# Three-block diffusion kernel: the opening reordered, thirds loaded from GpSimd, context normed a block ahead, unused products added

## The reference

```python
mod   = silu(c)     @ w_ada + b_ada        # six parts of 1024: shift, scale, gate, shift, scale, gate
mod_c = silu(c_ctx) @ w_ada + b_ada
h_l = rms_norm(x,   g_mix) * (1 + scale)   + shift
h_c = rms_norm(ctx, g_mix) * (1 + scale_c) + shift_c
p_l, p_c = h_l @ w_in, h_c @ w_in          # 1024 x 3072; the context needs only columns 1024 to 2559
mix = [fourier_mix(u), recurrent(q, v, gates, state of the context)] @ w_out
x = x + gate * mix
x = x + gate2 * experts(...)               # 16 experts, 32 tokens each, all their weights are read
```

## Time and profile before

| | |
|---|---|
| median of 3 runs | 2242.82 us |
| profiled execution | 2239.62 us, its span 2237.8 us |
| granted TensorE clock, mean | 0.859 |
| PE busy | 1707.0 us (76%) |
| VectorE, ScalarE, GpSimd busy | 808.9, 514.3, 60.8 us |
| DMA | 760.71 MB, mean 340 GB/s |
| chain that ended last | DMA 50%, PE 42%, DVE 5%, ACT 1%, issue 1% |

### The profile page before, as it was taken

How to read it: one execution, slowest core, us unless ns; L and a number is a source line. 1 busy time by engine, 2 the same in 40 slices (tenths; PEclk the granted TensorE clock), 3 DMA queues, 4 the chain that set the end, 5 groups by cost and what they waited for, 6 DMA issues and landing times.

```text
span 2237.8 us, 33889 instructions
## 1 busy us (share of the span) xinstructions
PE 1707.0 (76%) x14906; PEld 1183.2 (53%) x14906; DVE 808.9 (36%) x1271; ACT 514.3 (23%) x833; POOL 60.8 (3%) x94
## 2 busy tenths in 40 slices
PE   5999986656565665665765666665999999999997
PEld 4897752312222321331322222232898999998997
DVE  5766731000100100100010010010875789688877
ACT  2420210000000000000000000000673664365664
POOL 0015000000000000000000000000000000000000
PEclk8998988777778777887777877777999999999998
DMA  9776989999999999999999999999645659753541
GB/s 360 292 261 266 380 345 431 431 432 432 432 431 432 432 431 433 431 431 432 431 433 433 431 432 431 433 432 415 221 143 207 198 161 360 260 170 124 168 133 67
DMA packets 139014, 760.71 MB, mean 340 GB/s; under 512 B 7943, under 2 KB 96775, under 8 KB 106920
## 3 DMA queue, kind: packets, MB, share of 16 engines
q1 hardware_dynamic: 135256, 754.13, 83.5%
q10 hardware_dynamic: 3664, 5.24, 0.7%
HBM read 756.20 MB, written 3.14 MB: 339 GB/s over the span
## 4 chain that ended last, share of the span: by engine, by line
DMA 50%; PE 42%; DVE 5%; ACT 1%; issue 1%; SPq 0%; DVEq 0%; ACTq 0%
DMA arena<-in_w_exp_up 25%; DMA arena<-in_w_exp_gate 24%; PE ps L854 19%; PE ps L1171 6%; PE ps L1308 4%; PE ps L805 3%; PE ps L727 2%; DMA arena<-in_w_in 1%; PE ps L1006 1%; PE ps L1289 1%; PE ps L848 1%; DVE ring_lo L1734 1%; PE ps L1217 1%; PE ps L910 0%; PE ps L1228 0%
## 5 line engine op out<-in xcount | busy, mean ns | idle before, releaser
L1171 PE MATMUL ps<-arena,const 128*32 128x352 f32 x2816 | 334.7, 635 | 248.2 <-DMA arena<-in_w_exp_up 128.9
L1171 PEld LDWEIGHTS ps<-arena,const 128*32 128x32 f32 x2816 | 105.4, 141 | 465.4 <-DMA arena<-in_w_exp_up 163.8
L854 PE MATMUL ps<-u_hi,w_hi 128*128 128x258 f32 x960 | 277.3, 289 | 1.3 <-DVE ring_lo L1734 1.1
L1734 DVE TENSOR_TENSOR ring_lo<-ring,w_hi 128x1024 fp32r<-128x1024 f32 x217 | 263.8, 1219 | 31.1 <-ACT w_hi L1359 29.7
L2139 DVE TENSOR_TENSOR tail<-tail,ps 128x704 f32<-128x704 f32 x15 | 13.3, 888 | 720.6 <-PE ps L1171 720.6
L854 PE MATMUL ps<-u_lo,w_hi 128*128 128x258 f32 x960 | 272.9, 284 | 0.0
L854 PE MATMUL ps<-u_hi,ring_lo 128*128 128x258 f32 x960 | 269.2, 280 | 0.0
L1359 ACT ACTIVATE w_hi<-ring 128x1024 fp32r<-128x1024 f32 x217 | 227.1, 1051 | 55.4 <-PE ps L1308 34.6
L1171 PE MATMUL ps<-ring,const 128*32 128x352 f32 x1024 | 125.5, 654 | 80.6 <-DMA ring<-in_w_exp_gate 40.9
L854 PEld LDWEIGHTS ps<-u_hi,w_hi 128*128 128x128 f32 x960 | 181.6, 189 | 7.3 <-issue 5.2
L854 PEld LDWEIGHTS ps<-u_hi,ring_lo 128*128 128x128 f32 x960 | 183.3, 191 | 0.0
(11 more groups left out here) (317 smaller groups left out, 2435.4 us busy)
## 6 DMA issues: line engine op xcount, KB each, us to landing
arena<-in_w_exp_gate SPq DMA_DIRECT2D x45, 2816.0 KB, 35.2
ring<-in_w_exp_down SPq DMA_DIRECT2D x31, 3072.0 KB, 33.0
arena<-in_w_exp_up SPq DMA_DIRECT2D x32, 2816.0 KB, 35.8
ring<-in_w_in SPq DMA_DIRECT2D x37, 1536.0 KB, 7.0
arena<-in_w_exp_down SPq DMA_DIRECT2D x16, 3072.0 KB, 36.3
ring<-in_w_exp_gate SPq DMA_DIRECT2D x15, 2816.0 KB, 30.8
ring<-in_w_exp_up SPq DMA_DIRECT2D x15, 2816.0 KB, 30.3
ring<-in_w_ada SPq DMA_DIRECT2D x24, 1536.0 KB, 7.6
```

What stands on the lines that cost most here:

```text
L854: m = pe.matmul(ps[:, bank, 0:a.shape[-1]], w, a, start=(k == 0 and j == 0), stop=(k == KD - 1 and j == 2))
L1171: m = pe.matmul(ps[32 * j:32 * j + 32, bank + h, 0:FJ // 2], XCUR[:, k, :], SPACE[at][:, a:a + FJ // 2], start=(k == 0), stop=(k == KD - 1 ...
L1734: tt(slot(c["u"], KD, c["w"], of=LOW_SLOT)[:, :, at], slot(c["u"], KD, c["w"])[:, :, at], w_hi[:, s % HI, :, :].bitcast(F32), ALU.subtract ...
```

## The change

1. `in1`'s first unit gets its own place (`IN1_AT`, in `arena` at 13 K), outside the ring; its low parts are written in place. SP issues its load between ada units 5 and 6. TensorE does six ada units ahead of the context's sum of squares (`FIRST_ADA`), ScalarE the first three high parts ahead of the rows, VectorE all three low parts ahead of `mod_in(0)`. The context's modulation values and scale are formed behind x's chunks.
2. The thirds are issued by GpSimd, the first three when block 0 of `in1` is done, the fourth (which lies in the first unit's place) when that unit has been used, the others each when its buffer is free. The 24 that aren't gate thirds are used two items later than before.
3. In items 0 to 7 one chunk of context is normed by VectorE a block ahead and modulated by ScalarE (`modulated_context`), its low part is taken an item later.
4. `fill` puts a turn off to its next call; level 7 has a fill too.
5. Unused products: four behind `first_turn`, seven of 128 columns ahead of level 1, two behind the ada unit at `o_diagonal`, four ahead of each output projection of the third block.

```diff
 IN2_AT = 11
+IN1_AT = 7
...
-THIRD_AT = sorted([(3 + n, n % THIRDS, n // THIRDS) for n in range(THIRDS * KD)] +
+THIRD_AT = sorted([(5 + n, n % THIRDS, n // THIRDS) for n in range(THIRDS * KD)] +
                   [(i, THIRDS, k) for k, i in enumerate((8, 9, 10, 11, 14, 17, 20, 23))])
+FIRST_ADA = 6
...
-CTX_STEP = 2
-CTX_ITEMS = KD // CTX_STEP
+CTX_ITEMS = KD
...
-            u = self.unit(0, at=IN2_AT) if first else self.unit()
+            u = self.unit(0, at=IN2_AT) if first else self.unit(at=None if units else first_at)
...
+    plan.turn += 1
+    in1 = plan.dense(3072, lambda n: ["lat", "ctx"] if 8 <= n < 20 else ["lat"], [(8, 12)], first_at=IN1_AT)
...
-        THIRD1 = (ar(12 * K1, 1024), ar(13 * K1, 1024), ar(16 * K1, 1024), ar(17 * K1, 1024))
+        THIRD1 = (ar(12 * K1, 1024), ar(16 * K1, 1024), ar(17 * K1, 1024), ar(13 * K1, 1024))
...
+        SLOT[IN1_AT] = ar(13 * K1, UNIT)
...
+        LOW_SLOT[IN1_AT] = in1_lo
...
-            load_ada(0)
...
-                        sp.wait_ge(S("first_used"), n - len(THIRD1) + 1)
-                    sp.dma_start(THIRD1[n % len(THIRD1)], inp["w_ada"][0][k * P:(k + 1) * P, c0:c0 + 1024]).then_inc(
-                        S(f"first_in{n % len(THIRD1)}"), 16)
...
+            load_ada(0, range(FIRST_ADA))
+            first_view = inp["w_in"][0].rearrange("(k p) n -> p k n", p=P)
+            load(in1[0]["u"], slot(in1[0]["u"], KD, in1[0]["w"]), first_view[:, :, 0:in1[0]["w"]])
+            load_ada(0, range(FIRST_ADA, KD))
 
             def after_in1(i):
-                if i >= RING - 1:
-                    thirds_until(used_item[i - RING + 1])
...
-            load_dense(in1, inp["w_in"][0], after_in1)
-            for kc in range(RING):
-                if 5 + kc < len(used_item):
-                    thirds_until(used_item[5 + kc] - 1)
-                load_ada(2, [kc])
-            assert third_at[0] == len(THIRD_AT)
-            load_ada(2, range(RING, KD))
+            load_dense(in1[1:], inp["w_in"][0], lambda i: after_in1(i + 1))
+            load_ada(2)
...
-            def keep_warm(bank, k):
+            def keep_warm(bank, k, c0=0, c1=T):
...
-                    pe.matmul(ps[:, bank, 0:T], ones, const[:, 0:T], start=True, stop=True, skip_group_check=True)
+                    pe.matmul(ps[:, bank, c0:c1], ones, const[:, 0:c1 - c0], start=True, stop=True, skip_group_check=True)
...
-            for kc in range(4):
+            for kc in range(FIRST_ADA):
                 first_unit(kc)
             sum_squares()
-            for kc in range(4, KD):
+            for kc in range(FIRST_ADA, KD):
                 first_unit(kc)
             first_turn()
+            keep_warm(7, 4)
...
+            turning = []
+
             def fill(k):
 
+                while turning:
+                    turn(turning.pop())
                 for _ in range(k):
-                    if todo:
+                    if todo and not turning:
                         p, kc = todo.pop(0)
                         ada_unit(p, kc)
                         if kc == KD - 1:
-                            turn(p)
+                            turning.append(p)
...
             for n in range(LEVELS):
+                if n == 1:
+                    keep_warm(5, 7, 0, P)
                 if n >= 1:
                     pe.wait_ge(S("qk_ready"), n)
                     pe.wait_ge(S("level_out"), n)
...
-                fill(2 if n < LEVELS - 1 else 0)
...
             ada_unit(4, 0)
+            keep_warm(0, 2)
             pe.wait_ge(S("o_diagonal"), 1)
...
                 attention(raised_dense(in3[l], l == 0), in3[l], QA3, KA3)
+                keep_warm(6, 4)
                 dense(out3[l], OUT3_ORDER)
...
             root()
             root()
+            high_parts(starts["in1"] + 3)
             name, n = plan.used[ada[0][KD - 1]]
             act.wait_ge(S(name), n)
             mark(act.activation(ROWS0, ps[:, 6, :], ACT.Copy), "rows_out")
...
-            high_parts(starts["in1"] + 3)
...
+            def modulated_context(c):
+
+                act.wait_ge(S("normed"), KD + c + 1)
+                link(act.activation(HC[:, c, :], CTX[:, c, :], ACT.Identity, scale=scl[:, 2, c:c + 1],
+                                    bias=modc[:, c:c + 1]), "hc_chunk")
+                mark(act.activation(C_HI[:, c, :], HC[:, c, :], ACT.Copy), "x_high")
...
                     if done < CTX_ITEMS:
-                        for c in range(CTX_STEP):
-                            high_modulated(1, CTX_STEP * done + c)
+                        modulated_context(done)
...
-                if p == 0:
-                    link(tt(modc[:, 0:k].rearrange("p (j q) -> p j q", j=CG), v[:, :, :, 1], bias, ALU.add))
...
+            def context_in():
+
+                v = ps[:, 4, 0:64].rearrange("p (q j c) -> p j q c", q=4, j=CG)
+                link(tt(modc[:, 0:16].rearrange("p (j q) -> p j q", j=CG), v[:, :, :, 1],
+                        V("b_ada", 0, 16).rearrange("p (j q) -> p j q", j=CG), ALU.add))
...
-            low_parts(starts["in1"] + 2)
+            low_parts(starts["in1"] + 3)
             mod_in(0)
             scale_columns(V("g_mix", 0, 8), mod[:, 0, 8:16])
-            scale_columns(V("g_mix", 0, 8), modc[:, 8:16])
...
-            modulate_chunk(0, 0)
-            modulate_chunk(0, 1)
-            low_parts(starts["in1"] + 3)
...
+            modulate_chunk(0)
+            modulate_chunk(1)
             for c in range(KD):
                 if c + 2 < KD:
-                    modulate_chunk(0, c + 2)
+                    modulate_chunk(c + 2)
                 low_modulated(c, H, X_HI, X_LO)
+            context_in()
+            scale_columns(V("g_mix", 0, 8), modc[:, 8:16])
+
+            def norm_context(c):
+
+                link(tt(CTX[:, c, :], CTX[:, c, :], rs[:, 0:T], ALU.mult), "normed")
+
+            norm_context(0)
             for i, it in enumerate(in1_items):
                 low_parts(it["s"] + HI)
-                if i < CTX_ITEMS:
-                    chunks = range(CTX_STEP * i, CTX_STEP * i + CTX_STEP)
-                    for c in chunks:
-                        link(tt(CTX[:, c, :], CTX[:, c, :], rs[:, 0:T], ALU.mult), "normed")
-                    for c in chunks:
-                        modulate_chunk(1, c)
-                    for c in chunks:
-                        low_modulated(c, HC, C_HI, C_LO)
+                if i + 1 < CTX_ITEMS:
+                    norm_context(i + 1)
+                if 1 <= i <= CTX_ITEMS:
+                    low_modulated(i - 1, HC, C_HI, C_LO)
...
+            pool.wait_ge(S(in1_items[0]["done"][0]), in1_items[0]["done"][1])
+            for n, (_, c, kc) in enumerate(THIRD_AT):
+                c0 = ADA_PASS + 1024 * c if c < THIRDS else ADA_FIRST
+                if n >= len(THIRD1):
+                    pool.wait_ge(S("first_used"), n - len(THIRD1) + 1)
+                if n == len(THIRD1) - 1:
+                    pool.wait_ge(S(plan.used[in1[0]["u"]][0]), plan.used[in1[0]["u"]][1])
+                pool.dma_start(THIRD1[n % len(THIRD1)], inp["w_ada"][0][kc * P:(kc + 1) * P, c0:c0 + 1024]).then_inc(
+                    S(f"first_in{n % len(THIRD1)}"), 16)
```

31 lines of the change are left out of this document (9 added, 22 removed).

## The result

After: 2228.9 us median (2225.7 to 2229.0), against 2243.1 us (2241.5 to 2243.5) before; ratio 0.9938, 95% interval 0.9925 to 0.9952, which is 14.2 us. Forecast: 2226.1, 2218 to 2236. The profiled executions took 2239.62 before and 2228.90 after (span 2227.0), 10.7 us less; the rest of the 14.2 lies in how far single executions stray from their medians.

The account below looks back on a forecast made before the run. TensorE's order bounds the kernel before the expert stream, DMA within it, TensorE again after. Terms -3.9 - 1.3 - 4.8 - 6.0 - 0.2 - 0 - 0.5 = -16.7 us from the 2242.82 median give 2226.1, range 2218 to 2236.

Parts of the forecast that it names:

- A: Opening: with the first input unit loaded before ada units 6 and 7, input products start at 39.8, gain 3.9 us.
- B: Opening: four unused products behind the first turn keep the clock up in the first block group, gain 1.3 us.
- C: First input projection: spreading the context work removes TensorE's waits for VectorE's low parts, gain 4.8 us.
- D: First input projection: issuing the thirds from GpSimd's queue instead of SP's costs 0.
- E: Level stage: unused products ahead of level 1 and less thin work before level 3 save 6.0 us of clock.
- The turns: Level stage: turns put off no longer wait for ScalarE; net 0.2 us gained, from +1 to -1.9.
- rival 2: Early first unit wins little and transfers around 222 to 264 us come late: 2232 us, chance 0.08.
- F: Diagonal: two unused products ahead of it give zero, ends +1.4 and -0.9 us.
- G: Third model: four unused products before each output projection gain 0.5 us in all.
- Rivals 3 and 5: Expert stream absorbs the gain: 2242 us, chance 0.04; GpSimd feeds thirds too slowly, TensorE waits: 2260 us, chance 0.05.
- Rival 1: Level stage: the clock falls all the same or elsewhere, price 6.0 us: 2232 us, chance 0.18.
- Rival 4: Fillers and turn cost more than they give, with no clock won: 2238 us, chance 0.05.

Follow-up runs that it names:

- no fillers: The changed kernel with all four added sets of unused products taken out: 2228.6 us.
- turns back: The changed kernel with the turns directly behind their passes again and no ada units behind the last level: 2225.7 us.
- tuned: Changed kernel: ada load before expert half, last turn before s0 products, no fillers at level 1 and diagonal, eight unused products before third model's input; 2231.2 us.
- two buffers: The changed kernel with two instead of four buffers for the thirds that GpSimd loads: 2260.9 us.
- turns + load: The changed kernel with turns directly behind their passes, no ada units behind the last level, and one ada load issued ahead of an expert half: 2231.7 us.
- after again: The changed kernel measured once more with nothing edited: 2227.6 us.
- load first: The changed kernel with one ada unit's load issued ahead of an expert half on SP's queue: 2226.1 us.

## Why the prediction was right, and where it was not

The forecast of the median was 2.8 us low, that of the trace 6.0 us: 2222.9 against 2228.9. Part by part in the trace, 0.7 of it are in the start, 0.4 in the rest of in1 with its first unit, 3.5 between in1 and the experts, 1.4 behind them. That the median came closer is luck: the profiled execution of before was among its quicker ones.

*A, first unit: right.* Modulation forecast at 37.5, measured 37.44; start 39.8, measured 40.43 and 40.72. The missing 0.7 is the filler of B, which ended behind VectorE's first low part (39.63). Undone: 3.2 us in the trace, about 6 in the medians. That the forecast met the modulation to 0.1 us is in part luck: in the ten traces with this opening it is read between 36.65 and 39.36.

*B, filler at the opening: not shown.* Forecast 1.3; in the one trace without it the first unit takes 0.4 to 1.6 us longer than in the ten with it, but ends only 0.1 us behind the slowest of them. The total does not show it.

*C, context spread: right.* Forecast 4.8, measured 4.65 between the traces and 4.55 with C alone undone, where the median rose by 4.5 too. This is the part that the runs show best.

*D, thirds on GpSimd: right from before to after (nothing lost, 15.6 us of VectorE's waits in 9 times, no wait of TensorE), but "I price the move itself at nothing" leaves out what the later items ask of the queue.* With them the SP queue cost 4.8 us of in1 in the one trace that has it, and nothing in the median. Issued by GpSimd, a third landed in a median of 7.4 us, with VectorE busy 59.1 of the 78 us from 50 to 128; issued by SP in the variant, in 8.9. The Trainium skill, page "SBUF — State Buffer", section "SBUF: two separate sides", would have GpSimd held up while VectorE has the shared port, which it ties to certain modes of VectorE's operations; no view here tells the mode. An issue took 527 ns in the median and 752 at most, so this trace does not show it at a size that counts.

*E, level stage: the size near, the reason wrong.* Forecast 6.0 of clock; the clock lost in *levels* went from 8.5 to 3.4, 5.1. That the stage as a whole became 5.9 shorter (83.8 to 77.9) is another sum, which also holds what the late turns moved. The steps named were the filler ahead of level 1 and the thin stretch ahead of level 3. The first is refuted (no fillers: 76.6), the second as the sole cause too (turns back: 77.8 with no clock lost, 80.9 with 3.4). A kernel with both undone was not run, so that either of them is enough stays open; against it speak tuned, with late turns, and two buffers, with both, which lost 8.5 and 5.1. What is shown is that the order of work before the change lost 8.5 us twice, and ten of the other twelve traces lost 0 to 3.4. What decides it in a given program was not settled: two programs with the same order up to there lost 0.0 and 3.4 (turns back, turns + load). Up to the experts the clock gave back less: from the first product of the Fourier transform on 15.9 us were lost before, 11.2 and 12.1 in the two traces of after.

*The turns: the term whose parts behind the last level were too small.* Forecast: "Net 0.2 gained, from +1 to -1.9". Its named parts, -1.9, +1.2 and +1, add up to +0.3, and no ada unit moved past the last level: 80 recorded instructions of ada units lie between it and the experts before and after. The wait for ScalarE's rows went, but the last turn behind the last level makes VectorE read the modulation at 234.14 after an idle 1.61 [the rows of after above], and the output starts 6.88 us behind the last level instead of 5.28, +1.6 where 1 was forecast. Then comes the ada unit that TensorE waits 1.76 us for, with its transfer of 13.44 us. That was rival 2's mechanism ("an ada unit ... late by some 3 us"), at half its size. *To experts* is +3.2, of which the forecast had about 1. E and the turns together were to give 6.2 us up to the experts and gave 2.7 (after again 2.2); with that, the profiled run would have come out at 2225.4 against the 2222.9 that the sum gave. Whether putting the turns off costs or gains in the whole is not settled: turns back is 2.4 us shorter *to experts* and 1.9 faster in the median, load first is 1.9 us shorter than turns + load in both stretches and 5.7 faster.

*F and G: right, since they are near nothing.* F 0: the diagonal took 1.98 instead of 2.47, but with the fillers out it took 1.98 as well, behind a wait of 1.25 us for VectorE. G forecast 0.5; out3's first group lost 1.7 us of clock at 2058 in the first trace of before and at 2048 in the no-filler one, none in the second trace of before, and none in the eleven where the filler stands. From there to the end it takes 167.6 to 167.9 us with the filler and 167.8 to 168.0 without it, 0.3 between the first two traces.

*Signs.* One wait of 0.5 us for L1733, at the turned blocks; in1's last block ends at 149.8 (149 forecast); no wait at the two sums (L771 and L755 before); the stream's share of the DMA at 0.95 and more from 308 us in windows of 4 us, where before it was from 320: 12 us, though I had put the two at 302 and 318. Levels 1 and 3 at 3.8 was half right: 3.79 and 4.20, with level 2 at 4.88. The stream absorbed nothing: *rest* is 1913.5 to 1916 us in all kernels but one (tuned, 1917), whatever start the experts have, from 292.9 to 332.6 us. Rivals 3 and 5 are out. Rival 1 came in its second form, the clock fell elsewhere, but at less than its price: 3.4 lost where 8.5 had been. Rival 4 named something real, since the four fillers together give nothing in the median and the last turn cost more than its 1 us; its time of 2238 is out, since the levels became shorter all the same. Rival 2 came in part.

One slip in the prediction's bounds: the best ends of its terms add up to 23.4, not 24, which gives 2219.4 instead of 2218.5. Nothing hangs on it.

The median fell by 14.2 and the trace by 10.8, because single executions of the kernel before lay between 2235 and 2248 us in these measurements, those of after between 2226 and 2229. The profiled execution of before was among its quicker ones.

## What to carry to other kernels

A wait that VectorE sets in a stretch where TensorE is otherwise busy was the gain that held and could be forecast to a few tenths (context); take these first. A fall of the clock that one filler prevents may come a few microseconds later, as it did here at level 2: count clock lost over the whole stretch, not the level that got faster. Compare two orders of work only at equal clock lost, or over many executions: turns back looked better than the change in one pair and worse in the other. When work is put behind a late step "because nothing waits for it", follow its result to the engine that reads it and its slot to the transfer that it frees; here the output began 1.6 us later, and TensorE waited 1.8 us for the transfer. Taking that wait away brought the experts only 0.4 us forward.

## What the runs showed of the hardware that was not expected

The granted clock's falls in these stretches cost 1.7 us or a multiple: at the levels 0.0, 3.4, 5.1 and 8.5 in 14 traces; 1.7 in the third model's first group in eight traces, and between 1742 and 1754 us in four others; and 1.7 between 232 and 244 us in eight. A fall avoided at one place came at another in after and after again (192 to 200 or 184 to 192; 1936 or 1742) without an edit.

A trace with long waits lost more than their length: with two buffers TensorE waited 23.3 us in in1, 13.6 us of clock were lost there, and in1 ended 32.3 us later (182.83 against 150.49).

The filler ahead of level 1 shifted the fall and not its cost: level 1 took 4.99 to 5.95 us in all four traces without it and 3.7 to 3.8 in nine of the ten with it, while 3.4 us of clock were lost in *levels* in no fillers as in after.
